# Where the Fourier transform ends: the order of ScalarE's and VectorE's last steps before the projections w_a and w_b

## The reference

```
yx = (g_a * (fourier_mix(u[..., :512]) @ w_a) + g_b * (y_hgrn @ w_b)) @ w_out
x = x + mx[:, :, 2] * yx
...
m = rms_norm(mem, norm_mem_w)          # second block: memory of 256 rows
kv = m @ wkv                           # keys and values of cross attention
```

## Time and profile before

| | |
|---|---|
| median of 3 runs | 869.91 us (868.6 to 872.92) |
| profiled execution, its own time | 869.27 us |
| its span, first to last instruction | 867.5 us |
| busy: PE, DVE, ACT, POOL | 98%, 68%, 55%, 51% |
| mean granted TensorE clock | 0.996 |

### The profile page before, as it was taken

The page is one execution under the profiler, slowest core; times in us unless marked ns, Lnnn a source line. Parts: engine busy times, 40 slices in busy tenths (PEclk is TensorE's granted clock), DMA queues, the critical chain, the costliest instruction groups (busy, mean ns, idle before and its releaser), DMA issues.

```text
span 867.5 us, 15214 instructions
## 1 busy us (share of the span) xinstructions
PE 846.2 (98%) x6034; PEld 783.2 (90%) x6034; DVE 593.0 (68%) x1193; ACT 477.6 (55%) x794; POOL 443.5 (51%) x213
## 2 busy tenths in 40 slices
PE   7899999999999999999999999999999999999996
PEld 2388899999799999999999998999999899999996
DVE  4887979867667797676767779586448544544455
ACT  4542345442656665555555864555447666666665
POOL 4765512223652688888888300200000788888881
PEclk9999999999999999999999999999999999999999
DMA  9957565755376466555565545354536466656551
GB/s 341 367 216 251 177 231 194 231 171 188 126 237 206 131 190 198 180 187 182 183 186 179 161 147 194 98 180 124 182 98 195 132 199 179 196 178 197 184 170 49
DMA packets 45755, 160.89 MB, mean 185 GB/s; under 512 B 5218, under 2 KB 5490, under 8 KB 45556
## 3 DMA queue, kind: packets, MB, share of 16 engines
q1 hardware_dynamic: 45680, 159.91, 57.0%
q10 hardware_dynamic: 4, 0.01, 0.0%
HBM read 158.85 MB, written 1.05 MB: 184 GB/s over the span
## 4 chain that ended last, share of the span: by engine, by line
PE 85%; DVE 5%; ACT 3%; POOL 3%; DMA 2%; issue 1%; SPq 0%; ACTq 0%; DVEq 0%; POOLq 0%
PE bank L650 13%; PE bank L652 13%; PE bank L654 13%; PE bank L1017 9%; PE bank L1023 5%; PE bank L1058 4%; PE bank L1056 4%; PE bank L1054 4%; PE bank L916 2%; DVE wlo L510 1%; PE bank L744 1%; PE bank L746 1%; PE bank L743 1%; POOL wlo L510 1%; POOL xr L2304 1%
## 5 line engine op out<-in xcount | busy, mean ns | idle before, releaser
L510 POOL TENSOR_TENSOR wlo<-raw,whi 128x1024 fp32r<-128x1024 f32 (+1 forms) x174 | 405.8, 2351 | 374.3 <-ACT whi L1266 374.3
L1266 ACT ACTIVATE whi<-raw 128x1024 fp32r<-128x1024 f32 (+1 forms) x253 | 258.1, 1026 | 63.4 <-PE bank L654 27.1
L1692 DVE SCALAR_TENSOR_TENSOR accs<-bank,vec,accs 128x189 f32<-128x189 f32 (+4 forms) x440 | 161.2, 434 | 72.0 <-ACT accs L1556 72.0
L650 PE MATMUL bank<-h,whi 128*128 128x256 f32 x504 | 144.9, 288 | 0.0
L652 PE MATMUL bank<-h,wlo 128*128 128x256 f32 x504 | 143.5, 285 | 0.5 <-POOL wlo L510 0.5
L654 PE MATMUL bank<-h,whi 128*128 128x256 f32 x504 | 143.3, 284 | 0.0
L510 DVE TENSOR_TENSOR wlo<-raw,whi 128x1024 fp32r<-128x1024 f32 x79 | 95.5, 1221 | 17.8 <-ACT whi L1266 17.1
L652 PEld LDWEIGHTS bank<-h,wlo 128*128 128x128 f32 x504 | 97.5, 193 | 0.9 <-POOL wlo L510 0.7
L650 PEld LDWEIGHTS bank<-h,whi 128*128 128x128 f32 x504 | 97.5, 193 | 0.7 <-issue 0.3
L654 PEld LDWEIGHTS bank<-h,whi 128*128 128x128 f32 x504 | 97.4, 193 | 0.0
L1054 PE MATMUL bank<-gh,whi 128*128 128x256 f32 x320 | 90.7, 283 | 0.0
(11 more groups left out here) (342 smaller groups left out, 1857.3 us busy)
## 6 DMA issues: line engine op xcount, KB each, us to landing
raw<-in_up SPq DMA_DIRECT2D x88, 512.0 KB, 3.5
raw<-in_w_in SPq DMA_DIRECT2D x45, 512.0 KB, 4.1
raw<-in_down SPq DMA_DIRECT2D x44, 512.0 KB, 3.6
ada_kT<-in_adaT SPq DMA_DIRECT2D x22, 512.0 KB, 4.1
raw<-in_w_out SPq DMA_DIRECT2D x16, 512.0 KB, 4.2
raw<-in_w_in_t SPq DMA_DIRECT2D x12, 512.0 KB, 4.5
ada_vM<-in_adaT SPq DMA_DIRECT2D x10, 512.0 KB, 4.3
ada_buf<-in_adaT SPq DMA_DIRECT2D x8, 512.0 KB, 12.3
```

Source lines behind the costliest of these rows:

```text
L510: return e.tensor_tensor(wlo[:, j % HL, 0:k], raw[:, j % RAW, 0:k], whi[:, j % HL, 0:k].bitcast(F32), ALU.subtract)
L650: e.matmul(ps, wh[:, k, :], xh(k), start=k == 0, stop=False)
L1266: e.activation(whi[:, j % HL, 0:(k1 - k0) * 128], raw[:, j % RAW, 0:(k1 - k0) * 128], ACT.Copy).then_inc(S.hi.up(j))
L1692: return e.scalar_tensor_tensor(out=out, in0=a, scalar=s, in1=b, op0=o1, op1=o2)
```

## The change

ScalarE keeps memory steps 3 and 4 behind the copies of groups 0 and 1. The copies of groups 2 and 3 then follow each other, the four high halves `fmh` follow these, then the two high halves of the normed heads, then memory steps 5, 6 and 7. Before, `yb_high(0)` and step 5 stood behind the copy of group 2, and `yb_high(1)` behind that of group 3. VectorE makes the four `fml` ahead of the two `ybl`; before, it made the `ybl` first. TensorE's, GpSimd's and SP's streams are the same.

```diff
@@ act @@
             for g in range(4):
                 w.wait_ge(S.dft_mm, ("tok", g))
                 e.activation(M["PP"][:, g, :], lin_bank(("tok", g))[:, :], ACT.Copy).then_inc(S.fm.up(("PP", g)))
-                if g == 2:
-                    yb_high(0)
-                elif g == 3:
-                    yb_high(1)
-                if g < 3:
+                if g < 2:
                     w.wait_ge(S.on, (0, 3))
                     mem_step(3 + g)
             for g in range(4):
                 w.wait_ge(S.dft_mm, ("dim", g))
                 e.activation(M["fmh"][:, g, :], lin_bank(("dim", g))[:, 0:L], ACT.Copy).then_inc(S.fm.up(("hi", g)))
+            yb_high(0)
+            yb_high(1)
+            mem_step(5)
             mem_step(6)
             mem_step(7)
@@ dve @@
-            for n in range(2):
-                normed_low(n)
             for g in range(4):
                 w.wait_ge(S.fm, ("hi", g))
                 tt(M["fml"][:, g, :], lin_bank(("dim", g))[:, 0:L], M["fmh"][:, g, :].bitcast(F32),
                    ALU.subtract).then_inc(S.fml.up(g))
+            for n in range(2):
+                normed_low(n)
```

## The result

The changed kernel took 871.34 us (median of 20 runs, 869.78 to 875.82), the kernel before 869.13 us beside it (20 runs, 867.47 to 872.92). The ratio is 1.0027, with a 95% interval of 1.0017 to 1.0037: 2.3 us slower, 1.5 to 3.2, and less than 0.5%. The forecast was +1.79 us, and 871.7 us as a time.

What follows compares the result with a forecast made beforehand. It took TensorE, busy 98% of the span, as the bound. +0.90 us at w_a 2 and +0.89 at w_out 0 make +1.79, added to the median 869.91: 871.7 us, range 869.2 to 873.7.

Steps and rivals of the forecast that it cites:

- TensorE's start at the transform: At w_a 0: dim 3 no longer waits for the copy of group 3, so w_a 0 starts 1.55 us earlier.
- The wait for `ybl` 0: At the third matmul of w_b 0: TensorE loses 0.13 us, as `ybl` 0 ends at 229.36 and is wanted at 229.25.
- The memory step at 1.79 us: On ScalarE and GpSimd ahead of w_a 2: moved memory step 5 delays steps 6, 7 and all behind by 1.79 us.
- The wait at w_a 2: At w_a 2: TensorE waits 2.42 us for its halves and is then 0.90 us later than before.
- The chain to w_out 0: From w_a 2 to w_out 0: loads wait for earlier low halves, so w_out 0's low half comes 1.79 us later.
- No link of this waits for TensorE: Between w_a 2 and w_out 0: no load, high half or low half depends on TensorE, so all moves by 1.79 us.
- landings still longer: Rival, at the loads before w_out 0: landing grows by one more step of 0.8, making +2.6 us; chance 0.04.
- The clock: Rival, at w_a 2 and w_b 2: pauses lower TensorE's clock, +2.9 us on top of +0.90, 873.7 us; chance 0.06.
- Its own signs: Right: w_a 0 near 227.6, some 2.4 us wait at w_a 2. Wrong: clock under 1.00 in 234 to 240.
- The wait at L695: At w_out 0: a TensorE wait of about 1.5 us near 255 speaks for the forecast, one under 0.6 against.
- After w_out 0: Behind w_out 0: w_out 1 to 3 wait no more than before, and nothing of the lag is given back.

Runs made afterwards that it cites:

- the control: The kernel before, unchanged, timed and profiled once more as one of the kernels compared: ratio 1.0003 to the kernel before.
- VectorE's part alone: The kernel before with only VectorE's four `fml` moved ahead of the two `ybl`, ScalarE as before: ratio 0.9994 to the kernel before.
- step 5 put back: The changed kernel with memory step 5 again behind the copy of group 2, the two `ybh` still behind the `fmh`: ratio 1.0013 to the kernel before.
- the filler: The changed kernel with two matmuls of unused result added on TensorE ahead of w_a 2, to fill its wait: ratio 1.0031 to the kernel before.

## Why the prediction was right, and which of its terms were off

- **TensorE's start at the transform**: right in the trace shown, 1.73 against 1.55 forecast; w_a 0 followed dim 3 by 0.68, not by 0.86. It was taken from one execution, though. In the control the old order has no such wait, so this gain is there only where the memory lands late.
- **The wait for `ybl` 0**: there, 233.66 in the place of some 233.47; 0.2, forecast 0.13.
- **The memory step at 1.79 us**: right to 0.02. GpSimd's operation took 0.73 there, as the forecast took it, not 1.74.
- **The wait at w_a 2**: right to 0.01 us. The runs with two, three or no steps in front of w_a 2 show its cause: the low start is at 8.74, 10.54 and 5.84.
- **The chain to w_out 0**: right in the main as a mechanism. In the nine profiles with steps ahead of w_a 2, w_out 0's second matmul stands 19.7 to 21.0 us behind GpSimd's low start: 20.26 before, 19.74 in the control, 21.02 changed, and 20.33 with VectorE's part alone, where TensorE began 0.36 earlier. This time has three parts: until the load of w_out 0 is issued, 11.8 to 13.3; its landing, 4.0 to 4.5; and 3.6 for its two halves, the same in all nine. One sentence of the forecast failed, "No link of this waits for TensorE". In the changed kernel ScalarE makes the high halves of w_b 4 and w_b 5 behind `mh` 2 and `mh` 3, and both wait (2.16 and 1.46 us in the rows shown) for VectorE's sum over a chunk that TensorE has just ended.
- **The mis-sized terms** are the first two parts. The load of w_out 0 was issued 13.25 us behind the low start, where the forecast kept 12.69 from before, and landed in 4.16, not 3.96: 0.56 and 0.20. So it is +2.56 at w_out 0 between the two traces, where +1.79 was forecast. Two things went into the 0.56. The load of w_b 4, which the forecast never looked at, took 4.3 in both profiles of the changed kernel (3.4 before). And the clock fell: with step 5 put back, the same two landings (4.3 and 3.7) and a clock of 1.00, the first part took 12.72, so the clock is some 0.5 of the 13.25. With the filler, the clock up and w_b 4 landing in 2.7, it took 11.84. The rival "landings still longer", at +2.6 with a chance of 0.04, had this size, but by the landing of w_a 5, which was shorter here (3.8). Whether the change itself makes w_b 4 land later is open. Its load follows that of w_a 4 by 1.25 us, not 1.35, but the kernel with the filler and the control have the same spacing, and there it landed in 2.7.
- **The clock**: the rival was at 0.06, and the clock did fall behind w_a 2 in both profiles of the changed kernel. Its price was wrong: +2.9 was counted on top of +0.90, over 24 matmuls. The slow stretch lasted 3.4 us and held TensorE up by 1.5, and of these all but some 0.5 lay inside the wait at w_out 0.
- **Its own signs**: those for "right" at w_a 0, at w_a 2 and for the load of w_a 5 came. The wait at L695 was 0.7, not about 1.5, as TensorE was 1.58 later at w_out 0 than forecast. One sign for "wrong" came as well, the clock under 1.00 behind w_a 2.
- **After w_out 0** nothing was given back: 35.84 us to ffn_up against 35.86.
- **The median** is made of executions with early and late landings on both sides. The forecast's +1.79 lies in the interval, 1.5 to 3.2. That 871.7 comes so near to 871.34 is luck in part: it starts from 869.91, the median of three runs, which the 20 runs put at 869.13, and adds too little. By the two traces of before the loss at ffn_up is 2.5 or 4.0 us, the second outside the interval; how often each occurs was not counted.

## What to carry to other kernels

When a bound engine's wait is removed, look for what meets it next: here a ring of loads and halves that hardly goes by when the engine starts, and to which the same edit added 1.8 us. A moved step costs what stands behind it in its queue, counted with the wait on its partner (1.79, not the 1.25 of its own operations). And one trace is one draw: a wait behind a load whose landing varies by 2 us should be read in several executions before it is worked on.

## What the runs showed of the hardware that was not expected

- The same load, of 1 MB at the same place in the same instruction stream, landed in 5.3 to 7.1 us over thirteen profiles. A load of 256 KB (w_b 4) landed in 2.6 to 4.5 over all fourteen.
- The same pauses may or may not bring the clock down. Near 38, waits of 0.5, 0.5 and 1.6 us came with 6.8 us at the lower level (0.50) in the changed kernel's first profile, and in its second, with the same three waits, with 1.00 throughout. Behind w_a 2 the clock fell both times, for 3.4 us, after waits of 0.80 and 1.07; with matmuls in the first of the two, and 0.39 left of the second, it did not. The Trainium skill's "TensorE: Matmul & The Clock Gate", section "What's actually happening", calls the number of slow matmuls at a kernel's start "run-variable". No run here counts those; what varies here is the fall behind the waits near 38.
